# First expert's rows by one-hot products, the second half's modulation ahead of a weight split, gate rows moved

## The reference

```python
s1, sc1, g1, s2, sc2, g2 = adaln(cond, ada_w, ada_b)      # six rows of 1024
h = rmsnorm(x, norm1_g) * (1 + sc1) + s1
q, k, v = split(h @ w_qkv)                                 # layer 0
...
h = rmsnorm(x, norm2_g) * (1 + sc2) + s2                   # layer 1, ahead of the experts
probs = softmax(h @ w_router)
topv, topi = top_k(probs, 2); topv /= sum(topv)
gates = sum(one_hot(topi) * topv)
for e in range(8):
    out += gates[:, e] * swiglu(h, w_gu_e[e], w_down_e[e])
x = x + g2 * out
```

## Time and profile before

| what | value |
|---|---|
| median of three runs | 1435.17 us (1434.14 to 1436.02) |
| profiled execution | 1438.77 us |
| its span | 1436.9 us |
| PE busy | 1371.2 us (95%) |
| DVE busy | 1120.2 us (78%) |
| ACT busy | 819.8 us (57%) |
| POOL busy | 239.5 us (17%) |
| moved from and to memory | 406.06 MB |
| mean granted clock of TensorE | 0.980 |

### The profile page before, as it was taken

The page is one execution under the profiler, slowest core; times in us unless marked ns, Lnnn a source line. Parts: engine busy times, 40 slices in busy tenths (PEclk is TensorE's granted clock), DMA queues, the critical chain, the costliest instruction groups (busy, mean ns, idle before and its releaser), DMA issues.

```text
span 1436.9 us, 17409 instructions
## 1 busy us (share of the span) xinstructions
PE 1371.2 (95%) x6901; PEld 1155.5 (80%) x6901; DVE 1120.2 (78%) x1029; ACT 819.8 (57%) x824; POOL 239.5 (17%) x337
## 2 busy tenths in 40 slices
PE   4899979999999999988999999999999999999996
PEld 2687557799999986776898888988988889888894
DVE  2697765557777556566799899999998999989987
ACT  4422763532223223355677777777777777777773
POOL 4000580000000013000799500000000000000001
PEclk9999999999999999978999999999999999999998
DMA  9966443945454536526799999999999999999991
GB/s 310 356 214 238 141 147 127 320 154 168 149 182 147 187 139 215 181 103 240 272 364 381 368 413 372 367 412 341 404 373 369 412 373 372 393 344 409 365 412 67
DMA packets 118584, 406.06 MB, mean 283 GB/s; under 512 B 8130, under 2 KB 30835, under 8 KB 102115
## 3 DMA queue, kind: packets, MB, share of 16 engines
q1 hardware_dynamic: 111376, 382.24, 71.2%
q0 software_dynamic: 6048, 19.44, 4.6%
q10 hardware_dynamic: 1074, 3.23, 0.6%
HBM read 394.92 MB, written 9.96 MB: 282 GB/s over the span
## 4 chain that ended last, share of the span: by engine, by line
PE 90%; DVE 3%; DMA 2%; ACT 2%; issue 1%; POOL 1%; SPq 0%; POOLq 0%; ACTq 0%
PE ps L1756 26%; PE ps L1758 26%; PE ps L1757 26%; PE ps L2141 1%; PE ps L1951 1%; PE ps L1930 1%; PE ps L1769 1%; DMA raw<-in_w_qkv 1%; DVE ring_lo L1553 1%; PE ps L2052 1%; PE ps L1851 1%; DMA xg<-rows_dram,pick_to 1%; PE ps L1995 1%; PE ps L2132 1%; DMA lamv<-in_lambda_k 1%
## 5 line engine op out<-in xcount | busy, mean ns | idle before, releaser
L1553 DVE TENSOR_TENSOR ring_lo<-raw,ring_hi 128x2048 fp32r<-128x2048 f32 (+1 forms) x210 | 452.1, 2168 | 52.6 <-ACT ring_hi L1004 52.0
L1004 ACT ACTIVATE ring_hi<-raw 128x2048 fp32r<-128x2048 f32 (+1 forms) x210 | 381.3, 1819 | 130.3 <-PE ps L1758 127.6
L1756 PE MATMUL ps<-ring_hi,xe 128*128 128x512 f32 (+1 forms) x584 | 221.1, 379 | 1.7 <-issue 1.5
L1758 PE MATMUL ps<-ring_lo,xe 128*128 128x512 f32 (+1 forms) x584 | 218.5, 374 | 0.0
L1757 PE MATMUL ps<-ring_hi,xe 128*128 128x512 f32 (+1 forms) x584 | 218.4, 374 | 0.0
L1149 DVE TENSOR_TENSOR ring_lo<-raw,ring_hi 128x2048 fp32r<-128x2048 f32 x53 | 120.4, 2288 | 110.1 <-ACT ring_hi L786 110.0
L786 ACT ACTIVATE ring_hi<-raw 128x2048 fp32r<-128x2048 f32 x53 | 101.2, 1913 | 163.0 <-PE ps L1758 145.1
L1553 DVE TENSOR_TENSOR ring_lo_more<-raw,ring_hi_more 128x2048 fp32r<-128x2048 f32 (+1 forms) x70 | 151.7, 2168 | 18.6 <-ACT ring_hi_more L1004 18.4
L1004 ACT ACTIVATE ring_hi_more<-raw 128x2048 fp32r<-128x2048 f32 (+1 forms) x70 | 127.4, 1820 | 40.3 <-PE ps L1758 40.2
L1756 PEld LDWEIGHTS ps<-ring_hi,xe 128*128 128x128 f32 x584 | 111.0, 190 | 17.9 <-issue 1.8
L1758 PEld LDWEIGHTS ps<-ring_lo,xe 128*128 128x128 f32 x584 | 110.6, 189 | 16.1
(11 more groups left out here) (322 smaller groups left out, 2416.0 us busy)
## 6 DMA issues: line engine op xcount, KB each, us to landing
raw<-in_w_gu_e SPq DMA_DIRECT2D x128, 1024.0 KB, 8.0
raw<-in_w_down_e SPq DMA_DIRECT2D x88, 1024.0 KB, 8.9
raw<-in_w_gu_e SPq DMA_DIRECT2D x64, 768.0 KB, 6.9
raw<-in_ada_w SPq DMA_DIRECT2D x40, 1024.0 KB, 5.1
raw<-in_w_gu SPq DMA_DIRECT2D x44, 512.0 KB, 4.9
raw<-in_w_qkv SPq DMA_DIRECT2D x12, 1024.0 KB, 10.3
raw<-in_w_down SPq DMA_DIRECT2D x11, 1024.0 KB, 4.8
raw<-in_ada_w SPq DMA_DIRECT2D x16, 512.0 KB, 13.0
```

Source lines behind the costliest of these rows:

```text
L1004: act.activation(ehi[m % RINGM][:, 0:w], raw[:, (MOE_U0 + m) % RAW, 0:w], ACT.Copy).then_inc(hi_ready, 1)
L1553: dve.tensor_tensor(elo[m % RINGM][:, 0:w], raw[:, (MOE_U0 + m) % RAW, 0:w], ehi[m % RINGM][:, 0:w].bitcast(F32), ALU.subtract).then_inc(l ...
L1756: pe.matmul(out, l_hi, r_hi, start=first, stop=False)
L1758: return pe.matmul(out, l_hi, r_lo, start=False, stop=last)
```

## The change

Three things are rewritten.

1. For expert 0 there is no list and no gather. PE multiplies the kept rows with the one-hot matrix (`select_rows`): for each of eight blocks of channels, three products, one for each tile of tokens, straight into banks 0 and 1. `number_slots(0)` moves to the other experts' in `number_others`, and POOL's first gather is that of expert 1.
2. ACT's `split_hi(QKV0 + 2)` moves behind the first tile of the second half's modulation, DVE's `split_lo(QKV0 + 2)` behind its second tile.
3. The four gate pieces, which stood together behind the counts, are taken apart: the first ahead of the third tile's turns in `turn_normed(3)`, the second behind the place counts, the other two where they were. With them go ACT's `keep_gate` calls, ACT's `hi(RING - 1)`, now behind the first expert's upper parts, and DVE's order of `lo(1)`, `low_xe` and `lo(2)`. PE's wait for the last two pieces goes to the first product that writes into their banks.

```diff
-        GATE_BANKS = (7, 3, 4, 5)
+        GATE_BANKS = (7, 2, 4, 5)
...
-            pool.wait_ge(idx_first, 1)
             pool.wait_ge(rows_stored, 16 * TILES)
-            bring_rows(0)
             pool.wait_ge(idx_ready, 1)
             bring_rows(1)
...
                     first_high(hf, k)
+                    if (hf, k) == (1, 0):
+                        split_hi(QKV0 + 2)
 
             first_modulate(0)
             split_hi(QKV0 + 1)
-            split_hi(QKV0 + 2)
             first_modulate(1)
...
             modulate(3, 4, None)
+            keep_gate(3, 0, GATE_BANKS[0])
             for m in range(RING - 1):
                 hi(m)
...
-            hi(RING - 1)
-            for j in range(4):
-                keep_gate(3, j, GATE_BANKS[j])
+            keep_gate(3, 1, GATE_BANKS[1])
...
             for half in range(2):
                 high_xe(0, half, half)
+            hi(RING - 1)
+            for j in range(2, 4):
+                keep_gate(3, j, GATE_BANKS[j])
...
                     if k:
                         first_low(hf, k - 1)
+                    if (hf, k) == (1, 1):
+                        split_lo(QKV0 + 2)
...
             split_lo(QKV0 + 1)
-            split_lo(QKV0 + 2)
             first_norm(1)
...
-            dve.wait_ge(idx_ps, 1)
-            dve.tensor_scalar(pick_to[:, 0:1], numbers_of[:, 0:1, 0], -1.0, 0.0, ALU.add, ALU.max).then_inc(idx_first, 1)
             lo(1)
+            for half in range(2):
+                low_xe(0, half, half)
             dve.wait_ge(cnt_ps, 1)
             dve.tensor_copy(cnt[:], ps[:, 6, 96:96 + N_EXP]).then_inc(cnt_ready, 1)
             lo(2)
-            for half in range(2):
-                low_xe(0, half, half)
...
-            turn_normed(3)
+            turn_normed(3, lambda k: spread_gate(3, 0, GATE_BANKS[0]) if k == 2 else None)
...
             ins.then_inc(pos_ps, 1)
+            pe.wait_ge(rows_ready, 2)
+            spread_gate(3, 1, GATE_BANKS[1])
+
+            def select_rows():
+
+                pe.wait_ge(rows_ready, TILES)
+                pe.wait_ge(sel_ready, 1)
+                for half in range(2):
+                    for q in range(4):
+                        kc = 4 * half + q
+                        for k in range(TILES):
+                            ins = pe.matmul(ps[:, half, q * P:(q + 1) * P], rows[:, k, kc * P:(kc + 1) * P], choice[0][:, k, :],
+                                            start=(k == 0), stop=(k == TILES - 1))
+                    ins.then_inc(xe_ps, 1)
...
-                pe.wait_ge(xg_loaded, 16 * (e + 1))
+                pe.wait_ge(xg_loaded, 16 * e)
...
-            number_slots(0)
-            pe.wait_ge(idx_first, 1)
+            select_rows()
             for k in range(TILES):
                 ins = pe.matmul(ps[:, 6, 96:96 + N_EXP], ones[:].to_broadcast([P, P]), mask[:, k, :],
                                 start=(k == 0), stop=(k == TILES - 1))
             ins.then_inc(cnt_ps, 1)
-            pe.wait_ge(rows_ready, TILES)
-            for j in range(4):
+            for j in range(2, 4):
                 spread_gate(3, j, GATE_BANKS[j])
-            turn_gathered(0, 0)
-            pe.wait_ge(gbc_sb, 16)
+            pe.wait_ge(gbc_sb, 14)
 
             def number_others():
                 pe.wait_ge(cnt_ready, 1)
-                for e in range(1, N_EXP):
+                for e in range(N_EXP):
                     number_slots(e)
...
-                        if c == 0 and e:
-                            pe.wait_ge(y_sb, e)
+                        if c == 0:
+                            pe.wait_ge(y_sb, e) if e else pe.wait_ge(gbc_sb, 16)
```

More of the change, by code:

```diff
@@ L398, in build @@
             sem, ("tokT_ps", "rows_ready", "rows_stored", "zero_ready", "acc_zeroed"))
-        sel_ready, idx_ps, idx_first, idx_ready, selT_ps, selT_sb, xg_loaded, xe_ps, xe_hi_ready, xe_lo_ready = map(
-            sem, ("sel_ready", "idx_ps", "idx_first", "idx_ready", "selT_ps", "selT_sb", "xg_loaded", "xe_ps",
+        sel_ready, idx_ps, idx_ready, selT_ps, selT_sb, xg_loaded, xe_ps, xe_hi_ready, xe_lo_ready = map(
+            sem, ("sel_ready", "idx_ps", "idx_ready", "selT_ps", "selT_sb", "xg_loaded", "xe_ps",
                   "xe_hi_ready", "xe_lo_ready"))
@@ L727, in bring_rows @@
             def bring_rows(e):
-                if e:
+                if e > 1:
                     pool.wait_ge(xe_ps, 2 * e)
```

## The result

| | before | changed |
|---|---|---|
| median (5 runs each) | 1434.14 us | 1425.91 us |
| lowest to highest | 1432.84 to 1436.02 | 1424.04 to 1428.23 |
| profiled execution | 1438.77 | 1425.51 |
| its span | 1436.9 | 1423.7 |
| mean granted clock | 0.980 | 0.985 |

The ratio is 0.9942, with a 95% interval from 0.9927 to 0.9956: 8.3 us faster (6.3 to 10.5). The forecast was 12.8 us faster, 1422.4. The time lies in the range, but two thirds of the expected gain came. The two traces differ by 13.2 us in their spans, nearly the forecast; the question of this document is why the times of the runs differ by less.

A forecast was written before the change was run, and what follows sets the result against it. PE, busy 90% of 1436.9 us, was taken to bound the kernel, so gains lie where it waits or runs at its lower clock. 5.2 + 7.6 = 12.8 us off 1435.2 gave 1422.4, range 1417.5 to 1428.

The forecast's parts named there:

- the two holes: PE idle 3.42 us for the second half's modulation rows, and 4.80 us for expert 0's gathered rows at the experts' entry.
- Part one: Second half's modulation ahead of the third unit's split: PE's next unit starts at 54.7, not 59.87, 5.2 us earlier.
- The fold: End of the projection: DVE's last fold ends at 129.9, PE asks for it at 130.9, so it fits by 1 us.
- I take 5.2: Gain of the earlier modulation, taken to live to the end of the projection: 5.2 us, ends 3.5 and 5.4.
- Part two: Expert 0's rows by selection products instead of list and gather, gate rows moved: 7.6 us faster, ends 3.8 and 9.4.
- worth a start at 660.4: Old entry of the experts at 658.67 plus 1.73 us for slow first products; the new entry was forecast at 652.1.
- The selection, 6.0 us: Ahead of the experts: 24 products as 48 instructions, 5.3 us at 2.4 GHz, 10.6 at 1.2 GHz, taken as 6.0.
- The gate row ahead of the third tile, 1.5 us between 0.9 and 2.2: Gate row between second and third tile's turns, not in a wait: costs 1.5 us, and all that follows is late.
- 6 x 0.12 = 0.7: Expert 0's slot numbers, moved to the other seven's: six instructions cost 0.7 us there.
- The loads hold the experts: Rival, experts' stage: an earlier PE waits for loads, in the worst case losing all 7.6 us; 1424 to 1430, chance 0.10.
- The clock stays down: Rival, experts' entry: all added work runs at 1.2 GHz, PE enters at 659.7; about 1431.7 us, chance 0.08.
- Slower, the selection does not stream: Rival, selection: each of 48 instructions takes 0.464 us, 22.3 us instead of 6.0; 1438.7 us, chance 0.06.

The follow-up runs named there:

- second trace of before: The kernel before, run again with no edit: ratio 1.0004; its trace belongs to an execution of 1435.89 us.
- part one alone: The kernel before with only the second half's modulation put ahead of the third unit's split, measured twice: 1431.40 us (0.9982) and 1430.62 us (0.9969).
- the third: The kernel before, run once more with no edit for another trace, which belongs to an execution of 1438.48 us.
- measured alone: The changed kernel with the second half's modulation put back behind the third unit's split: 1428.79 us, ratio 0.9956 to the kernel before.

## Why the prediction was right, and where its sizes were off

**What bounds the kernel, and the two holes:** right. Both are gone in the trace. What has grown on PE's way is the row of slot numbers, below.

**Part one's first step, 5.2 us at the third unit:** right in size. PE asks for it at 54.09 and not at 59.87, 5.8 earlier; 0.6 of that was there already at a load of the modulation's weights, whose products start at 40.54 and not at 41.13 in this execution. The margin for the split was 0.4 us, where half a microsecond was forecast. At the attention nine traces with part one have a mean of 139.6, five without it 144.5: 4.9. The fold fitted by 1.1 us.

**"I take 5.2":** this is the first term that was over-sized. At the end four comparisons with and without part one give 2.6, 4.4, 2.0 (0.9956 against 0.9942) and 3.2 us, a mean of 3.1. Each of the four is uncertain by 1.5 to 3 us, the mean by an estimated 1 us: 5.2 is out, the lower end of 3.5 is not. The prediction followed the gain to the end of the projection and no further. Between the attention and the last normalisation the table has means of 478.5 with part one and 478.0 without: half a microsecond back, where the places at which the clock falls differ between executions. The other 1.3 us can't be found in the traces. Whether it is lost time at the lower clock or chance stays open.

**Part two, the entry "worth a start at 660.4":** this is the second. The gain of 8.3 at the entry (660.4 - 652.1) was right for executions like the second trace of before: 33.19 and 1.7 for the slow first products, against a mean of 26.2 in the six kernels with the selection and the numbers in one row, 8.7. Against the two traces of part one alone, where the gather is 2.4 us quicker and the first products run at the full clock, it is 32.7 - 26.2 = 6.5. Whether part one itself shortens the entry, or these two executions happened to have a short one, five traces don't tell. One trace had been taken for the rule, and of the three of before it is, with the third, on the long side. The sum of part two's upper end gives 9.3 and not 9.4, on which nothing hangs.

**The selection, 6.0 us:** it took 5.43 (637.12 to 642.55), at the full clock as assumed, 0.113 apiece. The row that priced it, 27 products of 256 columns, was the right one.

**The gate row ahead of the third tile, 1.5 us between 0.9 and 2.2:** 0.86 in the trace of the changed kernel (621.47 to 622.33), 1.7 in that of the doubled selection (621.95 to 623.66, at the lower clock). The bounds hold. The place counts' gate row was hidden, as forecast: the wait left behind it is 0.31.

**"6 x 0.12 = 0.7" for the numbers of expert 0:** this is the third. Six more products in a long row of tiny ones don't cost their own time alone, by the mean of the traces: from the first expert product to the hidden rows the six kernels take 37.1 us, part one alone 35.5, a difference of 1.6. A single trace says little here, since the six go from 34.9 to 38.2. The first trace of before, less its 1.7 at the slow entry, has 35.5 as well.

With 3.1 for part one, and 6.5 - 1.6 = 4.9 to 8.7 - 1.6 = 7.1 for part two (measured alone: 6.3), the sum is 8.0 to 10.2, and the measured 8.3 lies in it. The forecast of 12.8 took the long execution's gain from the median of all: the difference of the two traces, 13.2, does agree with it. But that agreement is in part luck. By the columns of the table the forecast was 5.2, 0, 6.6 and 1.0 us, and the two traces differ by 5.8, -1.4, 9.8 and -0.9. The entry came out 3.2 us shorter than forecast, 26.7 and not 29.9, with the clock falling 10.2 us into the stretch (628.0) and not 2.6 (624.8), as in the trace of before; that made up for what was lost ahead of it and behind it.

**The rivals.** *The loads hold the experts:* no; the last column is 741.0 in every trace, and ACT waited 1.2 us for loads in all of it. The rate is 381 GB/s in the middle of the stage:

```profile
800.00:900.00 100.00, 100.00 (x481) 86.39 (x480) 90.95 (x53) 74.47 (x50) 3.51 (x2) 1.00 1.00 381
```

The Trainium skill, "DMA: Bandwidth & Descriptors", Specifications, has about 358 GB/s for a core; the trace's 381 is above it. The same page's section on bandwidth says that this is the share while both cores of a memory domain stream, and that a core alone measures more, so for this program on one core the figure was no bound. *The clock stays down:* not in the selection, the counts or the gate rows, where it was 1.00; in part yes behind them, at the numbers. *Slower, the selection does not stream:* no, 0.113 apiece.

## What to carry to other kernels

Before a gain is worked out from one trace, look how its length stands to the median, and at which stage the difference can lie: here the stages with waits and tiny products varied by up to 3.3 us from one execution to the next, the dense last one by 0.2, and a saving in the former is worth what the usual execution loses there. A gather of rows that are still on the chip can be a product with a one-hot matrix: here 48 instructions at 0.11 us took the place of a list, a gather and eight turns, for 5 to 7 us net. A row of tiny products that looks like waste may stand in a wait: see what the next dense product waits for before taking it apart.

## What was not expected of the hardware

One program's granted clock falls at different places in different executions: 1.00 in one trace of before and 0.72 in another over six microseconds of the last normalisation, with nothing changed in the program. The gather of the same rows took 6.7 and 7.1 us in the two traces of part one alone, and 8.1 to 9.1 in three of before, most of the difference in POOL's instruction: where DVE was running a split as it began, it ended 0.94 us after that split. Against that, the last 741 us of the kernel repeat to 0.2 us in fourteen traces.
